# Pool's program in another order: the prompt bias table and the window copies after the activation differences of a two-layer decoder step

## The reference, cut to what matters

```
y = conv_mixer(rmsnorm(h), state_conv, ...)          # layer 0
h = h + y
f = rmsnorm(h); h = h + (silu(f @ w_gate) * (f @ w_up)) @ w_down     # dense, D_FF = 2816
h = h + sigmoid(rmsnorm(h) @ ple_gate) * (p @ ple_proj)
# layer 1: compressed, selected and window attention over paged caches
blocks = rows.reshape(b, nc, 32, ...);  einsum('bnlgcd,lgcde->bngce', blocks, w_cmp)
logits = q k^T + rel_bias[bucket(q_pos - k_pos)]     # the bias table of the prompt's windows
new_buf = concat(state_win, new rows)[:, t:]         # returned as win_sample
```

## Time and profile before

| | before |
|---|---|
| median of 3 runs | 1313.13 us |
| the profiled execution | 1318.54 us, span 1316.1 us |
| PE busy | 1226.3 us, 93% of the span |
| DVE, ACT, POOL busy | 36%, 21%, 14% |
| share of PE in the chain that ended last | 88% |
| granted TensorE clock, mean | 0.97 of full |
| DMA | 326.42 MB, 248 GB/s over the span |

### The profile page before, as it was taken

How to read it: one execution, slowest core, us unless ns; L and a number is a source line. 1 busy time by engine, 2 the same in 40 slices (tenths; PEclk the granted TensorE clock), 3 DMA queues, 4 the chain that set the end, 5 groups by cost and what they waited for, 6 DMA issues and landing times.

```text
span 1316.1 us, 38823 instructions
## 1 busy us (share of the span) xinstructions
PE 1226.3 (93%) x16260; PEld 1012.6 (77%) x16260; DVE 473.7 (36%) x1382; ACT 275.5 (21%) x740; POOL 179.9 (14%) x318
## 2 busy tenths in 40 slices
PE   7999999999999998998777868889999999999998
PEld 5887887999999976485344456687897888989966
DVE  2111115668774321004676674421221211311321
ACT  1000003101000111135865852210010011010020
POOL 3012121012330002042243340000000000000000
PEclk9999999999999998997987989999999999999999
DMA  9787789996334464264485686688988989889810
GB/s 320 292 299 268 268 309 268 229 365 239 125 133 176 148 262 155 95 145 128 133 262 177 219 262 222 259 329 309 389 315 326 363 314 382 331 313 389 311 62 32
DMA packets 108320, 326.42 MB, mean 248 GB/s; under 512 B 15496, under 2 KB 33737, under 8 KB 106484
## 3 DMA queue, kind: packets, MB, share of 16 engines
q1 hardware_dynamic: 90868, 263.71, 54.1%
q0 software_dynamic: 16128, 59.94, 15.0%
q10 hardware_dynamic: 1152, 0.30, 0.1%
HBM read 316.64 MB, written 14.52 MB: 252 GB/s over the span
## 4 chain that ended last, share of the span: by engine, by line
PE 88%; DVE 7%; issue 2%; ACT 2%; DMA 0%; ACTq 0%; DVEq 0%
PE bank L1886 22%; PE bank L2447 15%; PE bank L1988 12%; PE pbank L2458 6%; PE bank L2024 6%; PE bank L1942 5%; PE pbank L2447 3%; PE bank L2458 3%; PE bank L2429 3%; PE bank L2097 2%; PE bank L2228 1%; PE bank L2062 1%; PE bank L2416 1%; PE bank L2222 1%; PE bank L2183 1%
## 5 line engine op out<-in xcount | busy, mean ns | idle before, releaser
L1886 PE MATMUL bank<-aT,gring 128*128 128x288 f32 x896 | 226.0, 411 | 3.5 <-DVE aT L1236 3.5
L1886 PEld LDWEIGHTS bank<-aT,gring 128*128 128x128 f32 x896 | 171.3, 192 | 52.2 <-issue 4.8
L2447 PE MATMUL bank<-X,gring 128*64 128x96 f32 x4608 | 194.4, 246 | 3.8 <-issue 3.8
L2447 PEld LDWEIGHTS bank<-X,gring 128*64 128x64 f32 x4608 | 191.5, 137 | 7.2 <-issue 7.1
L2458 PE MATMUL pbank<-Q,X 128*32 128x256 f32 x1152 | 78.3, 379 | 0.1
L1988 PE MATMUL bank<-aT,gring 128*128 128x144 f32 x528 | 72.3, 287 | 0.0
L1808 DVE TENSOR_TENSOR hT<-hT,bank 128x288 f32<-128x288 f32 x48 | 18.9, 449 | 145.7 <-PE bank L2416 145.7
L1942 PE MATMUL bank<-Q,X 128*64 128x64 f32 x2048 | 63.3, 223 | 7.9 <-issue 7.9
L1942 PEld LDWEIGHTS bank<-Q,X 128*64 128x64 f32 x2048 | 61.3, 138 | 11.9 <-issue 11.9
L1988 PEld LDWEIGHTS bank<-aT,gring 128*128 128x128 f32 x528 | 68.1, 191 | 0.0
L1815 DVE TENSOR_TENSOR X<-X,bank 128x96 f32<-128x96 f32 x72 | 18.4, 256 | 137.8 <-ACT X L1186 137.3
(11 more groups left out here) (362 smaller groups left out, 1765.1 us busy)
## 6 DMA issues: line engine op xcount, KB each, us to landing
gring<-in_moe SPq DMA_DIRECT2D x176, 512.0 KB, 5.6
Q<-in_moe SPq DMA_DIRECT2D x72, 512.0 KB, 6.9
gring<-in_dense_gu SPq DMA_DIRECT2D x44, 512.0 KB, 11.8
Q<-in_cache_cmp POOLq DMA_DIRECT2D x64, 256.0 KB, 5.8
Q<-in_cache_cmp SPq DMA_DIRECT2D x64, 256.0 KB, 5.7
gring<-in_conv_in SPq DMA_DIRECT2D x24, 512.0 KB, 9.8
gring<-in_dense_down SPq DMA_DIRECT2D x16, 704.0 KB, 5.4
gring<-in_ple_gate SPq DMA_DIRECT2D x16, 512.0 KB, 6.1
```

What stands on the lines that cost most here:

```text
L1886: ins = pe.matmul(bank(label, k)[:, 0:T], tile[:, 128 * i:128 * i + 128], rhs[:, i, :], start=i == 0, stop=i == C - 1)
L2447: ins = pe.matmul(m_bank(i, M_GU + f)[64 * w:64 * w + 64, CAP * u:CAP * u + CAP], gslot(("m", 0), 2 * f + u)[:, o:o + 64], ae[:, c, :], st ...
```

## The change

Pool's instructions stay the same, all 875 rows of them; their order and two waits change. No other engine's program changes.

- The write of `bias_rows` waits in addition for pair 2 to be done on PE (`full(pool, ("fb", 2))`).
- The 11 rounds of subtractions come right behind it. The read of `tabP`, the memset, the two copies and the eight window copies come after them.
- The reload of `w_cmp` waits for the last gate product of the embedding, ("pg", 0, 7), instead of ("norm", 2).

```
--- before.py
+++ after.py
@@ -778,23 +778,9 @@
                               (pmask, "pmask"), (pT, "p"), (esum[:, :], "esum")):
                 pool.dma_start(dst, A[name]).then_inc(rest_in, 16)
             drained(pool, ("bv",))
+            full(pool, ("fb", 2))
             pool.dma_start(bias_rows, bvs[:, 0:ROW].unsqueeze(1).to_broadcast([HEADS, 128, ROW])).then_inc(bias_out, 16)
             pool.wait_ge(bias_out, 16)
-            shifted = bias_rows
-            shifted = bass.AP(shifted.tensor, 127, [[ROW - 1, 128], [128 * ROW, HEADS], [1, 256]])
-            full(pool, ("cv", B - 1))
-            pool.dma_start(tabP_, shifted).then_inc(bias_in, 16)
-            pool.wait_ge(bias_in, 16)
-            pool.memset(tabC[:, 0, 4:8, :], NEG).then_inc(blocks_ready, 1)
-            pool.tensor_copy(tabC[:, 0, 0:4, :], tabP[:, :, 159:256:32].rearrange("p h n -> p n h")).then_inc(blocks_ready, 1)
-            pool.tensor_copy(tabC[:, 1, :, :], tabP[:, :, 31:256:32].rearrange("p h n -> p n h")).then_inc(blocks_ready, 1)
-
-            for b in range(B):
-                n = (WIN - STEPS) * 512
-                src = A["state_win"][b, STEPS:WIN, :].rearrange("s n -> (s n)").rearrange("(a n) -> a n", a=16)
-                dst = O["win_old"][b].rearrange("s n -> (s n)").rearrange("(a n) -> a n", a=16)
-                pool.dma_start(dst, src).then_inc(win_stored, 16)
-
             for f in range(FC):
                 if f == 0:
                     pool.wait_ge(hff_ready, FC)
@@ -807,7 +793,22 @@
                 pool.wait_ge(hff_sums_ready, 4 * f + 3)
                 pool.tensor_tensor(hff_sums[2][:, f, :], hff[:, FC + f, 0:HT], hff_sums[1][:, f, :],
                                    ALU.subtract).then_inc(hff_sums_ready, 1)
-            full(pool, ("norm", 2))
+            shifted = bias_rows
+            shifted = bass.AP(shifted.tensor, 127, [[ROW - 1, 128], [128 * ROW, HEADS], [1, 256]])
+            full(pool, ("cv", B - 1))
+            pool.dma_start(tabP_, shifted).then_inc(bias_in, 16)
+            pool.wait_ge(bias_in, 16)
+            pool.memset(tabC[:, 0, 4:8, :], NEG).then_inc(blocks_ready, 1)
+            pool.tensor_copy(tabC[:, 0, 0:4, :], tabP[:, :, 159:256:32].rearrange("p h n -> p n h")).then_inc(blocks_ready, 1)
+            pool.tensor_copy(tabC[:, 1, :, :], tabP[:, :, 31:256:32].rearrange("p h n -> p n h")).then_inc(blocks_ready, 1)
+
+            for b in range(B):
+                n = (WIN - STEPS) * 512
+                src = A["state_win"][b, STEPS:WIN, :].rearrange("s n -> (s n)").rearrange("(a n) -> a n", a=16)
+                dst = O["win_old"][b].rearrange("s n -> (s n)").rearrange("(a n) -> a n", a=16)
+                pool.dma_start(dst, src).then_inc(win_stored, 16)
+
+            full(pool, ("pg", 0, C - 1))
             for k in range(4):
                 pool.dma_start(wc[:, 32 * k:32 * k + 32, :], A["w_cmp"][:, 32 * k:32 * k + 32, :]).then_inc(wcmp_again, 16)
```

More of the change, by code:

```diff
@@ L780, in _ @@
             drained(pool, ("bv",))
+            full(pool, ("fb", 2))
             pool.dma_start(bias_rows, bvs[:, 0:ROW].unsqueeze(1).to_broadcast([HEADS, 128, ROW])).then_inc(bias_out, 16)
             pool.wait_ge(bias_out, 16)
+            for f in range(FC):
+                if f == 0:
+                    pool.wait_ge(hff_ready, FC)
+                pool.tensor_tensor(hff_sums[0][:, f, :], hff[:, f, HT:T], hff[:, f, 0:HT], ALU.subtract).then_inc(hff_sums_ready, 1)
+                pool.wait_ge(hff_ready, FC + f + 1)
+                pool.wait_ge(hff_sums_ready, 4 * f + 1)
+                pool.tensor_tensor(hff[:, f, HT:T], hff[:, FC + f, HT:T], hff[:, f, HT:T], ALU.subtract).then_inc(hff_sums_ready, 1)
+                pool.tensor_tensor(hff_sums[1][:, f, :], hff[:, FC + f, HT:T], hff_sums[0][:, f, :],
+                                   ALU.subtract).then_inc(hff_sums_ready, 1)
+                pool.wait_ge(hff_sums_ready, 4 * f + 3)
+                pool.tensor_tensor(hff_sums[2][:, f, :], hff[:, FC + f, 0:HT], hff_sums[1][:, f, :],
+                                   ALU.subtract).then_inc(hff_sums_ready, 1)
             shifted = bias_rows
```

## The result

The changed kernel takes 1326.4 us (median of 4 runs, 1324.12 to 1333.09), against 1313.77 us for the kernel before (4 runs, 1310.99 to 1317.96). The ratio is 1.0109, 95% interval 1.0084 to 1.0134. It is slower by 12.6 us of medians. The profiled execution took 1324.12 us, its span 1321.3 us.

What follows compares the result with a forecast made beforehand. PE, busy 93% of the span, was taken to bound the kernel. Bias write 0, window copies' pause 10.9, clock 1.7 and reload 0 gave +12.6 us on 1313.13, so 1325.7 us, range 1309 to 1331.5.

Steps and rivals of the forecast that it cites:

- The write of the bias rows: Write moved behind pair 2: same 2.7 us PE pause and 1.7 us of clock, only later; change 0.
- The bound of -4.3: Lower bound, in us, for the bias write's move: the backlog is thinner, as tiles share it.
- The table's read: Moved behind the subtractions: issued at 385.5 us, landed at 393.5, so window copies are issued from 394.7.
- The window copies: Moved to 395 us, they starve the down projection's tiles; PE idle from 415.35 to 426.2, 10.9 us.
- The clock: Lower PE clock after the pause in the down projection: 1.7 us more, upper bound 3.0.
- The reload: Reload of `w_cmp`, moved from 456.6 to 495 us: 0 at both places, bounds -0.5 and +2.
- the pause in the pairs goes as well: Rival: small packets thin the write's backlog, so PE runs through the pairs, -4.3 us; 1321.4 us, chance 0.14.
- Fair shares: Rival: copies and down tiles share by halves, third tile lands at 410.5, no pause; 1313.1 us, chance 0.11.

Runs made afterwards that it cites:

- e6: The kernel before with only the write of the bias rows moved, behind pair 3; 1309.72 us.
- e7: The kernel before with only the write of the bias rows moved, behind pair 0; 1316.53 us.
- e4: The changed kernel with each window copy laid out as 16 x 16 pieces of 4064 bytes instead of 16 of 65 KB; 1311.33 us, ratio to before 0.9993.
- e5: The kernel before with only the reload of the compress weights moved, behind the last gate product of the embedding; 1305.66 us, one execution.
- e9: The kernel before with the bias write in four transfers, window copies in 4064-byte pieces and the reload moved; 1312.31 us against 1314.96, ratio 0.9983.
- e3: The kernel before with only the table's read and three small operations behind the subtractions, so the window copies follow the write at once; 1325.96 us, one execution.
- e2: The kernel before with only the eight window copies moved behind the subtractions; 1316.24 us, one execution.

## Why the prediction was right

**The direction and the sum.** +12.6 us was forecast and +12.6 us is between the medians, but the sum is right in part because two errors cancel. By terms:

**The write of the bias rows: the step that failed.** I wrote that the write lasts longer than two intervals, "so wherever it starts one packet meets it in full", and took 0, with an "issue" wait near 270. There was none. A packet of instructions was held indeed (due 253.5, came at 266.4), but for 13 us, while the one of the kernel before was held 16.3 and PE bears 13.6. The due times of the prediction were 1.5 us late, since they were counted back from a packet at 259.5 that had itself been held; so its 15 us for the first hold were too few, and the small distance to what PE bears was not seen. The hold is not of one length over the write, as e6 and e7 show. The rival named this case, "a hold of 12 instead of 15 us is enough"; its reason, that tiles thin the backlog, was not tested. The bound of -4.3 was right for the first profile; over four profiles the term is -2.9.

**The table's read.** 8.0 us forecast, 8.95 measured, and the three small operations 1.7 us instead of 1.15. The copies start 1.5 us later against PE than reckoned.

**The window copies.** The place, the third tile and the mechanism were as forecast: a tile gets a turn per packet, whatever the packet's size, and e4 shows it with nothing but the size changed. The pause was mis-sized, 13.8 for 10.9 us: 1.5 us from the later start, 2.0 from copies that took 30.9 us and not 28.95 (391.46 to 422.4), less 0.4 since the third tile came 2.2 us after them and not 2.6. 10.9 + 1.5 + 2.0 - 0.4 = 14.0. DVE waited 30.3 us, until 422.9, and not about 20: its wait is for the second tile, which the prediction itself had at 424.5, and the 20 us are those of the first.

**The clock.** 1.7 forecast, 5.00 - 2.86 = 2.1 us measured. The 1.7 came from the one profile of five in which the clock fell after the pause in the pairs.

**The reload.** 0 forecast; no wait came with it (e5, e9), and what the clock does there is not settled.

With the measured sizes, 13.8 + 2.1 - 2.9 = 13.0 us. That the forecast meets the medians to 0.1 us is luck: the main pause was set 2.9 us too short, and the pairs gave back 2.9 us that the sum had at 0. Of the rivals, "the pause in the pairs goes as well" is what happened, with 0.14 of the chances; its time was set too low because the main pause was. "Fair shares" happened in e4, where it was made to.

## What to carry to other kernels

A transfer that nobody waits for can still stop the kernel, if its packets are large or slow: what counts is when the buffers beside it run short. Put it where the loads are several steps ahead of their use, not where they are double buffered, or cut it into pieces of the size of the loads' own packets. Two such transfers in a row seem to need time between them for the ring to refill, as far as one profile (e3) shows.

## What the runs showed of the hardware

- Queues take turns by packet: beside a copy from DRAM to DRAM in rows of 65 KB the tiles had 230 packets to its 224, but 1.21 MB to its 7.28 in 24 us; with the copy in pieces of 4 KB (packets of 7.2 KB in the mean) they had 753 to 835 packets and 3.79 MB in 26 us.
- A long transfer of 4.6 KB packets at 0.69 us each held another queue's packet for 13 to 16 us where that came due 2 to 7 us after its start, and for 9 to 14 where it came due 15 us in or later; cut into four with a wait between, it held such packets 3 to 6 us and stopped nothing.
- PE's instructions come through the same engines, one block each 14.9 us in this stage, and PE stood still in the middle of a product in six profiles, in which a block was held for 13.9 to 16.3 us, and not in four in which it was held 12.6 to 13.2. The trace calls this "issue", as it does a wait for DVE's weight sums.
- After a pause of 14 us the clock stood at the lower of its two levels, 1.2 GHz, for some 4 us of work. It had fallen 4 us into the pause. After pauses of 2.7 (before), 3.9 (e2) and 5.8 us (e3) it fell too, after those of 2.4, 2.1, 1.6 and 1.0 us it did not.
